# Expert rows of a mixture-of-experts stage summed on the chip for all 32 experts instead of the last two

## The reference, cut to what matters

```
logits = h @ w_router + b_router            # (320, 32)
top_v, top_e = top_k(logits, 4)             # 4 experts of 32 for each token
gate = softmax(top_v)
for the rows x of expert e (those tokens that chose it):
    gu = x @ w_gu[e] + b_gu[e]              # (rows, 2048), 8 MB of weights
    gt, up = split(gu); gt = min(gt, 7); up = clip(up, -7, 7)
    act = gt * sigmoid(1.702 * gt) * (up + 1)
    out = act @ w_dn[e] + b_dn[e]           # (rows, 1024), 4 MB of weights
y[token] = sum over its 4 experts of gate * out
x = x + y ; result = rmsnorm(x) * norm_final
```

## Time and profile before

| | us |
|---|---|
| device time, median of 3 | 1360.87 |
| span of the profiled execution | 1356.19 |
| what lies around the span, by the median | 4.68 |
| PE busy / PEld busy | 1264.1 / 570.1 |
| DVE busy / ACT busy / POOL busy | 459.0 / 230.7 / 123.2 |
| chain of waits: PE / DMA | 74% / 23% of the span |
| bytes by DMA | 479.33 MB |

### The profile page before, as it was taken

One profiled execution on the slowest core, in us unless ns is written; L12 is line 12 of the kernel. 1 busy time (PEld: TensorE's weight loads), 2 busy tenths in 40 slices (PEclk: granted clock), 3 DMA queues, 4 the chain that ended last, 5 costly groups with the idle time before them and its releaser, 6 DMA issues.

```text
span 1356.2 us, 14399 instructions
## 1 busy us (share of the span) xinstructions
PE 1264.1 (93%) x5895; PEld 570.1 (42%) x5895; DVE 459.0 (34%) x809; ACT 230.7 (17%) x333; POOL 123.2 (9%) x164
## 2 busy tenths in 40 slices
PE   7999999999999999999999999999987778878786
PEld 5756766666543333333333333333322223222231
DVE  2897322211463322223113313222422222233226
ACT  4102432310221111111011111111211111111121
POOL 3110100000010100000000000100010000000020
PEclk9999999999999999999999999999999999999898
DMA  9715826465699999999999999999999999999994
GB/s 331 258 63 157 266 76 156 155 248 204 254 364 426 425 426 426 426 425 427 426 425 427 427 427 424 425 427 425 424 427 425 425 427 425 425 426 426 424 388 153
DMA packets 97115, 479.33 MB, mean 353 GB/s; under 512 B 43962, under 2 KB 46026, under 8 KB 72311
## 3 DMA queue, kind: packets, MB, share of 16 engines
q1 hardware_dynamic: 84641, 459.36, 83.3%
q0 software_dynamic: 11008, 15.63, 3.3%
q10 hardware_dynamic: 1374, 3.02, 0.6%
HBM read 477.57 MB, written 22.61 MB: 369 GB/s over the span
## 4 chain that ended last, share of the span: by engine, by line
PE 74%; DMA 23%; issue 1%; DVE 1%; ACT 0%; DVEq 0%; ACTq 0%
PE PS L1762 29%; PE PS L1400 15%; PE PS L1795 14%; DMA ring<-in_w_dn 12%; DMA ring<-in_w_gu 11%; PE PS L1340 4%; PE PS L1580 4%; PE PS L1624 3%; PE PS L1436 2%; PE PS L1847 1%; PE PS L1667 0%; PE PS L1527 0%; DMA XX<-in_x_prompt 0%; PE PS L1546 0%; PE PS L1644 0%
## 5 line engine op out<-in xcount | busy, mean ns | idle before, releaser
L1762 PE MATMUL PS<-ring,arena 128*64 128x512 f32 x1824 | 405.7, 597 | 39.2 <-DMA ring<-in_w_gu 27.6
L1251 DVE TENSOR_TENSOR arena<-PS,XX 128x1024 f32<-128x1024 f32 x32 | 39.2, 1224 | 659.2 <-PE PS L1762 659.2
L1762 PEld LDWEIGHTS PS<-ring,arena 128*64 128x64 f32 x1824 | 129.2, 139 | 293.7 <-issue 291.1
L1795 PE MATMUL PS<-ring,arena 128*64 128x512 f32 x896 | 203.7, 604 | 16.9 <-DMA ring<-in_w_dn 15.6
L1400 PE MATMUL PS<-arena,ring 128*128 128x320 f32 x768 | 213.5, 434 | 0.1
L1400 PEld LDWEIGHTS PS<-arena,ring 128*128 128x128 f32 x768 | 144.3, 190 | 58.7 <-issue 2.0
L1762 PE MATMUL PS<-arena 128*64 128x512 f32 x608 | 136.3, 595 | 11.6 <-DMA arena<-in_w_gu 10.8
L854 ACT ACTIVATE arena<-arena 128x1024 f32<-128x1024 f32 x32 | 33.9, 1058 | 618.4 <-DVE arena L1254 618.4
L554 POOL DMA_INDIRECT y_rows<-arena x60 | 59.8, 996 | 791.7 <-ACT arena L835 762.9
L1795 PEld LDWEIGHTS PS<-ring,arena 128*64 128x64 f32 x896 | 62.0, 139 | 142.0 <-issue 142.0
L1340 PEld LDWEIGHTS PS<-ident,arena 128*128 128x128 f32 (+3 forms) x580 | 63.1, 142 | 54.8 <-issue 49.0
(11 more groups left out here) (216 smaller groups left out, 670.2 us busy)
## 6 DMA issues: line engine op xcount, KB each, us to landing
ring<-in_w_gu SPq DMA_DIRECT2D x96, 2048.0 KB, 27.9
ring<-in_w_dn SPq DMA_DIRECT2D x48, 2048.0 KB, 29.3
arena<-in_w_gu SPq DMA_DIRECT2D x31, 2048.0 KB, 28.7
arena<-in_w_dn SPq DMA_DIRECT2D x16, 2048.0 KB, 30.0
ring<-in_w_in SPq DMA_DIRECT2D x11, 2048.0 KB, 11.3
ring<-in_w_mem_kv SPq DMA_DIRECT2D x2, 2048.0 KB, 20.7
ring<-in_cache_mem_k SPq DMA_DIRECT2D x32, 128.0 KB, 3.3
ring<-in_cache_mem_v SPq DMA_DIRECT2D x4, 1024.0 KB, 6.1
```

Of the source, the lines that this page charges most:

```text
L1251: nc.vector.tensor_tensor(gbuf[:], PS[:, 0:2, :], g_bias, ALU.add).then_inc(main["g_added"], 1)
L1762: last = mm(PS[64 * h:64 * h + 64, 2 * g + b, :], in_block(xT[:, k, :], b), (spare[kk] if m == BONUS else moe_ring(m, 2)[:, kk]) [:, g * D ...
L1795: last = mm(PS[64 * h:64 * h + 64, 4 + b, :], actT[:, b, j, c * BLK:(c + 1) * BLK], moe_ring(m, 4)[:, j, h * 512:(h + 1) * 512], start=c = ...
```

## The change

All 32 experts take the way over one-hot matrices; `y_rows`, its zeroing, the scatters, the reading of ranks and the rank sums on VectorE go away. The one-hot matrices no longer need TensorE: gates and positions are turned once, at the start (`turn_places`), into rows by expert (`RG`), and for each expert VectorE spreads its row over the partitions and compares it with the slot number (`gate_weights`: one shuffle of 128x640, two operations of 128x320), which gives `W` at once in the layout slot by token. TensorE then runs `to_tokens` for expert e-2 inside the gate-up of expert e: token tiles 0 and 1 after chunk 1, tile 2 after chunk 2. VectorE adds each tile's PSUM sum to the tokens (`add_tokens`, three adds per expert). Group e-2's sums use PSUM banks 6 and 7 (tile 0), 4 and 5 (tile 1) and 6 (tile 2), the same banks as the transposes and the down products, so each has to be read out before the next use. Second blocks of chunks 2 and 3, and of 4 and 5, are now joined behind one branch each; chunk 2's place is freed with chunk 3, chunk 4's with chunk 5. The activations' transposes move from behind the down products into the next expert's gate-up, after chunk 0. `h_rows` now holds whole rows in their own order, and the transposes read them with a stride.

```diff
     e, c = STREAM[m]
-    if c == 3:
+    if c in (2, 3):
         return "gu_done", NE, e + 1
-    if c == 5:
+    if c in (4, 5):
         return "dn_done", NE, e + 1
...
-        def scatter(v, e):
-            pool.wait_ge(main["zs_ready"], NE * v + e + 1)
-            for b in range(2):
-                nc.gpsimd.indirect_dma_start(
...
+        def add_tokens(v, g, tt):
+            i = GROUPS * v + g
+            dve.wait_ge(main["tok_done"], TT * i + tt + 1)
+            if i:
+                dve.wait_ge(main["tok_added"], TT * (i - 1) + tt + 1)
+            add_sums(tt, g == NE - 2).then_inc(main["tok_added"], 1)
+
+        def gate_weights(v, e):
...
+            nc.vector.stream_shuffle(RGs[:], RG, mask=[e] * 32).then_inc(main["rows_spread"], 1)
+            dve.wait_ge(main["rows_spread"], n)
+            for b in range(2):
+                last = nc.vector.scalar_tensor_tensor(W[e % 2][:, b, :], RGs[:, 0, :], slotpos[:, b:b + 1], RGs[:, 1, :],
+                                                      ALU.is_equal, ALU.mult)
+            last.then_inc(main["w_ready"], 1)
...
-        for r in range(TOPK):
-            j = TOPK - 1 - r
-            dve.wait_ge(yr_in[r], 32)
...
+        def block_sum(e, tt, b, start, stop, last):
+            for h in range(2):
+                ins = mm(token_sum(tt, h, last), W[e % 2][64 * h:64 * h + 64, b, tt * P:tt * P + ROWS[tt]],
+                         Zs[64 * h:64 * h + 64, b, :], start=start, stop=stop)
+            return ins
...
+                def between(c):
+                    if n == 0 and c == 0:
+                        first_list()
+                    if e and c == (1 if n == 1 else 0):
+                        turn_act(v, e - 1)
+                    if e >= 2 and c in (1, 2):
+                        tiles = range(2) if c == 1 else (2,)
+                        if c == 1:
+                            pe.wait_ge(main["actT_ready"], n)
+                            pe.wait_ge(main["zs_ready"], n - 1)
+                            pe.wait_ge(main["w_ready"], n - 1)
+                        else:
+                            pe.wait_ge(main["tok_added"], TT * (GROUPS * v + e - 2) + 1)
+                        if n == 2:
+                            for tt in tiles:
+                                bias_sum(tt)
+                        to_tokens(v, e - 2, counts[e - 2], tiles, n > 2, False, main["tok_done"])
...
+        pe.wait_ge(cnt_ready, 1)
+        most = pe.value_load(maxi[0:1, 0:1], min_val=0, max_val=T)
+        window(0)
         with pe.If(most > WIN):
...
-        with pe.Else():
-            last_experts()
-            pe.nop()
+        last_tokens(0, bd_done)
```

568 lines of the change are left out of this document (232 added, 336 removed).

## The result

The changed kernel takes 1421.47 us (median of 4 runs, 1419.42 to 1423.73) against 1360.52 us for the kernel before (4 runs, 1358.02 to 1361.69): a ratio of 1.0452, interval 1.0433 to 1.0471, so 61 us slower. 1413 us was predicted. The profiled execution has a span of 1418.0 us, 61.8 us more than before. Its own time is 1419.79 us, 1.8 us around the span, and every run listed with its span has 1.7 to 1.9 us there. The span of before, 1356.19 us, therefore belongs to the execution of 1358.02 us and not to one of 1360.9 us.

A forecast was written before the change was run, and what follows sets the result against it. TensorE was taken to bound the kernel until near 970 us, DMA after. Gate-up 17 at 967.9, eight experts at TensorE's pace to 1187.4, DMA's pace to 1386.9, tail to 1409.0, plus 4.7: 1413 us, range 1388 to 1430.

The forecast's parts named there:

- Gate-up of expert 17 ends at 967.9: Up to expert 17: added TensorE work of 1.3 + 3.0 and 65.8 us of groups moves its end from 897.8.
- The strided reading of tokens and of `XN` I take at nothing: At the start and in token transposes: reading operands at a stride costs nothing, -1 to +1 us.
- Experts 18 to 25 at 26.25 us: Eight experts after expert 17 go at TensorE's pace, 210.0 us, before it waits for transfers; reaches 1187.4 us.
- Then DMA's 29.9 us each: Experts 26 to 31 at DMA's pace, 179.4 us; last gate-up ends at 1366.8, last landing 1383.3, products 1386.9.
- Copy and far branch, 8.1 us: After the last products: result-row copy 1.0 us, latency 0.1, then 7 us for the branch over further windows; reaches 1395.0.
- First tile at half clock, 1.9 us: In the last sums: the first tile's 4 records take 1.9 us instead of 0.95, at 1.2 GHz; reaches 1396.9.
- 12.05 us to the end: From the first add to the span's end, as before, 12.05 us: reaches 1409.0, with 4.7 us around the span.
- A: Whole kernel: DMA sets the time throughout and TensorE's new work is free; 1332 us, faster; chance 0.04.
- B: Same mechanism, but groups cost columns alone (2.6 and 5.2 us) and the end branch is hidden; 1388 us; chance 0.16.
- C: In the expert loop: a new wait on TensorE, likely for VectorE's adds or from branch waits; 1446 us; chance 0.08.
- step 5: After the last products: the branch over further windows costs 7 us, bounds 0 and 9.1, with DMA queues empty there.

The follow-up runs named there:

- e5: Changed kernel with normed and fetched rows in k-major order again (contiguous operands) and the third tile's norm in two halves: 1411.96 us, ratio 1.0394.
- e2: Kernel before with rows whole and read at a stride of 8, third tile's norm in one piece; scatters and rank sums kept: 1368.36 us, ratio 1.0072.
- e6: Changed kernel with the far branch taken before the last expert instead of after its products: 1419.48 us, ratio 1.0450.
- e8: Kernel before without the scatters, the reads of rank rows and the rank sums, nothing put in their place: 1343.58 us, ratio 0.9890.
- e3: Changed kernel with every to_tokens and last_tokens matmul cut to 1 moving column instead of 512, same instruction count: 1373.56 us, ratio 1.0108.
- e12: Changed kernel with each to_tokens group replaced by one 1-column matmul a tile, without count branch or half-array form: 1364.23 us, ratio 1.0040.
- e4: Changed kernel with every to_tokens matmul issued twice into the same sum: 1492.97 us, ratio 1.0984.
- e10: Changed kernel with VectorE's making of each expert's gate matrix (shuffle and two masks) done three times: 1424.07 us, ratio 1.0474.
- e9: Changed kernel with the far branch taken before expert 28's gate-up, four experts before the end: 1419.5 us, ratio 1.0444.
- e11: Changed kernel with k-major rows, the third tile's norm in two halves, and the far branch before expert 28: 1408.35 us, ratio 1.0375.
- e1: Changed kernel with normed and fetched rows in k-major order again, third tile's norm still in one piece: 1415.61 us, ratio 1.0411.

## Why the prediction was nearly right

It named the right mechanism and came out 8 us short, inside its range. Step by step, on the time line of the profiled execution:

1. *Gate-up of expert 17 ends at 967.9.* It ended at 975.7, 7.8 us late: expert 1's gate-up starts 10.46 us later than before where 1.3 were taken, which is 9.2, and the loop up to there gave 1.4 back. The term that failed is "The strided reading of tokens and of `XN` I take at nothing", with its bounds of -1 to +1 us; e5 gives it as 8.0 us, e2 as 9.8. It was argued from transposes that read at the same stride. The time of a set of eight hides what the stride does to their loads, and rows of the kernel before show it:

```profile
L1340 PEld LDWEIGHTS PS<-ident,arena 128*128 128x128 f32 x560 | 61.2, 142 | 54.2 <-issue 48.6 <-DVE arena L1267 3.0
...
L1340 PEld LDWEIGHTS PS<-ident,XX 64*128 64x128 f32 x8 | 1.0, 199 | 0.0
```

The first row is of the whole kernel and has mostly contiguous operands, 142 ns a load; the second, from 355 to 395 us, is the third tile of X at a stride, 199 ns. What is loaded there is 64x128, the tokens, and what moves is 64x64, the identity: in a transpose too the strided rows are the stationary operand. The turned tokens of the changed kernel went the same way, from 140 to 195 ns:

```profile
L1261 PEld LDWEIGHTS PS<-ident,arena 128*128 128x128 f32 x8 | 0.9, 140 | 0.8 <-issue 0.8
...
L1261 PEld LDWEIGHTS PS<-ident,arena 128*128 128x128 f32 x8 | 1.0, 195 | 0.8 <-issue 0.8
```

(activations at 1075.45 us, contiguous; tokens at 1090.16, at a stride.) A set of eight pays only 0.07 us for it. In `first_tokens` the loads went from 191 to 335 ns and sixteen of them from 1.86 to 3.90 us, and TensorE's granted clock fell to 0.50 besides. No run shows why transposes pay so much less. On this the Trainium skill had a rule that I should have weighed ("SBUF — State Buffer", in the section on the DMA port swizzle): SBUF is read in lines of 16 bytes, and an access pattern that takes only one value from a line pays for it; 8 values of 4 bytes are two lines apart. The trace agrees that such a pattern costs (335 against 191 ns, and 195 against 140 in transposes); by how much, the rule does not say. The other terms: `turn_places` 2.0 us more than before from start to start (1.3 taken); groups 2.93 and their breaks nearly as worked out.
2. *Experts 18 to 25 at 26.25 us.* The pace came out, and the first wait for a chunk is the 0.56 us before 1177.60 us, ahead of expert 25. The count of eight is partly luck: it is the upper end of the step's own estimate (seven from the 10 us that it takes as likely), and issue to landing was 12.2 us in the median from 940 to 985 us. One expert fewer would have been 3.7 us more.
3. *Then DMA's 29.9 us each.* Four experts from 1232.19 to 1352.29 are 30.0 each. The last gate-up ended at 1375.9 (1366.8 predicted), 9.1 late, of which 7.8 are step 1's. What failed besides is the end of the step: only the last chunk's products were put behind the last landing (1391.0), without expert 30's sums. These wait for ScalarE's copy (1.52 us) and stand before both of the last down chunks, so the products ended at 1397.8, 3.2 us later than the landing asked for.
4. and 5. *Copy and far branch, 8.1 us.* TensorE stood for 5.93 us, so 2.1 less; I had taken 7 for the branch, between 0 and 9.1. e6 shows what belongs to the branch: with it gone from there 2.02 us are left for the copy (1.1 taken), so it added 3.9.
6. *First tile at half clock, 1.9 us.* 2.1.
7. *12.05 us to the end.* 12.1. Around the span the median has 3.5 us, 4.7 taken. Neither is a time that an execution spends there, which is 1.8 us: the rest is how far the median lies above the profiled execution, 2.9 us before and 1.7 after. The forecast took the profiled execution's time for the median's, and that 1.2 us came off the miss is luck.

Sum of the misses, rounded: 7.8 + 1.3 at the last gate-up, less 1.4 that the last transfers gave back (1391.0 against 1383.3), + 3.2 - 2.1 + 0.2 = 9.0 of the span, less 1.2 around it.

The bill by experiments, in us over before: rows gone -14.9 (e8); columns +46.8 (e3); the groups' branches, form and instructions +9.3 (e12 against e3); stride and whole norm +8.0 (e5); and 12.3 left for the bias sums (3.0), `turn_places` (2.0) and the tail's branch and half clock, which are not measured singly and needn't add up exactly, since each is hidden differently when another is away.

Of the rivals, A (DMA throughout, TensorE's work free) fell with the first stretch, 476.00 of 476.00 us and a share of 0.89. The Trainium skill's rule that spoke for it ("Perfetto Trace Analysis", Identifying the Most-Contended Engine: judge TensorE by its weight-load share and its share of peak arithmetic, not by matmul busy time) would have misled in the half of it that was looked at: the weight-load share was 35% (167 of 476 us) in a stretch in which the unbroken chain shows TensorE to be the bound. (e3 and e4 show what its columns cost over the whole span.) B (small prices) is refuted by the 3.30 us of a group with its breaks and the 5.93 us gap, C by e10. A's price for the part removed, 29.8 us, is itself twice what e8 gives.

## What to carry to other kernels

Work that is moved from DMA to an engine is paid for at the engine's price wherever the engine is the later of the two, and the DMA time saved counts only in the other stretches: here 47 us and more of columns for 15 us of transfers. Ask of every operand whose layout a change turns how long its weight loads take at that stride, in just the kind of instruction that will read it: the transposes hid a price of 0.07 us a set, and the matmuls with the same operand took twice their time. And a branch over code that is far away costs its gap and the half clock after it; moving it to where waits lie behind it moved the gap but brought nothing that the times show (e6, e9; 2.6 us at most in e11 against e5).

## What the runs showed of the hardware that was not expected

- In `first_tokens` a load of 128 stationary columns of f32 took 191 ns contiguous and 335 ns at a stride of 8 elements (32 bytes), in the changed kernel and in e2, and sixteen took 3.90 us at either level of the clock; in transposes it took 140 and 195 ns, and a set of eight 1.02 and 1.09 us.
- In all nine profiles with the strided loads the granted clock was 0.50 from 376 to 384 us, though TensorE counts as busy all the while; with contiguous loads and a gap of about 0.6 us ahead it stayed 1.00 in three (before, e5, e11) and fell in one (e8, 3.0 us late by expert 1), and with contiguous loads and a gap of 1.61 us it fell as well (e1). So every profile with strided loads has a fall that otherwise comes in some executions; what decides it is open.
- A late phase ahead of a stretch that DMA bounds is not absorbed: 10 us late at the start were 9.8 us late at the end (e2).
- The gap at the far branch was 9.06 us in the kernel before and in e8, 4.81 in e6, 4.97 in e11, and 5.93 in the changed kernel. DMA's share in it was 1.01 before and in e6, 1.03 in e11 and 0.04 in the changed kernel. So the load on DMA doesn't set its length, as step 5 had assumed, and an idle DMA doesn't make it vanish; what sets it is open.
